# One block behind each mixer: attention of a head between the half groups of the next heads' query projection

## What is computed

```python
x = x + mix                                   # mix ends in a product with the mixer's wo
q = (rmsnorm(x, norm_xattn) @ xa_wq)          # four heads of 256
p = softmax(q @ mk.T * 256 ** -0.5)           # over 256 memory tokens, for each head
x = x + (p @ mv) @ xa_wo
h = rmsnorm(x, norm_ffn)
x = x + (silu(h @ w1) * (h @ w3)) @ w2
```

## Time and profile before

| | |
|---|---|
| median of three runs | 3963.66 us (3962.3 to 3965.55) |
| profiled execution, its time | 3961.41 us |
| its span, first to last instruction | 3959.6 us |
| mean granted clock of PE, of full speed | 0.944 |
| PE busy | 3509.9 us, 89% |
| DVE, ACT, POOL busy | 39%, 28%, 15% |

### The profile page before, as it was taken

How to read it: one execution, slowest core, us unless ns; L and a number is a source line. 1 busy time by engine, 2 the same in 40 slices (tenths; PEclk the granted TensorE clock), 3 DMA queues, 4 the chain that set the end, 5 groups by cost and what they waited for, 6 DMA issues and landing times. The chain is left out here.

```text
span 3959.6 us, 62416 instructions
## 1 busy us (share of the span) xinstructions
PE 3509.9 (89%) x26745; PEld 3302.5 (83%) x26745; DVE 1546.4 (39%) x2408; ACT 1124.8 (28%) x2089; POOL 603.4 (15%) x859
## 2 busy tenths in 40 slices
PE   9899576986999999998899884765987999999998
PEld 8888465976999999996598784664986999999997
DVE  6345433333332232235326667445324333232233
ACT  6223235212321121124535521444302321121123
POOL 2000030100210010012312357320100111010011
PEclk9999797998999999998899997897998999999999
DMA  7322101221211111113656576854121211111111
GB/s 229 86 64 65 74 17 53 65 83 55 43 49 49 43 49 48 44 44 111 211 164 209 194 187 133 214 122 108 52 94 44 59 43 49 48 44 49 44 44 64
DMA packets 479601, 340.98 MB, mean 86 GB/s; under 512 B 108142, under 2 KB 455502, under 8 KB 476078
## 3 DMA queue, kind: packets, MB, share of 16 engines
q1 hardware_dynamic: 425082, 298.49, 26.4%
q10 hardware_dynamic: 43876, 18.99, 1.9%
q0 software_dynamic: 10368, 19.51, 1.5%
HBM read 241.40 MB, written 95.61 MB: 85 GB/s over the span
## 5 line engine op out<-in xcount | busy, mean ns | idle before, releaser
L83 PE MATMUL ps<-ff_h,ff_wh 128*128 128x352 f32 x4224 | 1009.3, 322 | 0.0
L83 PEld LDWEIGHTS ps<-ff_h,ff_wh 128*128 128x128 f32 x4224 | 730.3, 188 | 1.3
L83 PE MATMUL ps<-y_parts,ff_wh 128*128 128x352 f32 x2880 | 694.7, 323 | 16.9 <-DVE ff_wl L1069 16.9
L83 PE MATMUL ps<-ff_h,ff_wl 128*128 128x352 f32 x2112 | 676.5, 320 | 0.0
L83 PEld LDWEIGHTS ps<-y_parts,ff_wh 128*128 128x128 f32 x2880 | 504.5, 189 | 17.2 <-DVE ff_wl L1069 17.2
L83 PE MATMUL ps<-y_parts,ff_wl 128*128 128x352 f32 x1440 | 466.0, 324 | 0.0
L83 PEld LDWEIGHTS ps<-ff_h,ff_wl 128*128 128x128 f32 x2112 | 396.0, 187 | 0.0
L1213 DVE TENSOR_TENSOR x<-ps,x 128x352 f32<-128x352 f32 x240 | 125.8, 524 | 483.8 <-PE ps L83 480.9
L1453 POOL TENSOR_TENSOR ff_silu<-ff_silu,rs 128x352 f32<-128x352 f32 x132 | 126.8, 962 | 1229.5 <-ACT ff_silu L1392 1229.5
L83 PE MATMUL ps<-rw_parts,rw_wh 128*128 128x352 f32 (+1 forms) x1152 | 289.6, 333 | 25.4 <-PEq L2502 13.7
L83 PEld LDWEIGHTS ps<-y_parts,ff_wl 128*128 128x128 f32 x1440 | 271.8, 189 | 0.0
(11 more groups left out here) (370 smaller groups left out, 5462.5 us busy)
## 6 DMA issues: line engine op xcount, KB each, us to landing
ff_w<-in_ffn_w SPq DMA_DIRECT2D x120, 512.0 KB, 3.8
mixed_t<-oq_st SPq DMA_DIRECT2D x48, 176.0 KB, 1.9
rw_ra_d<-tb_rk SPq DMA_DIRECT2D x8, 1056.0 KB, 8.2
rw_kbt_d<-tb_gk SPq DMA_DIRECT2D x8, 1056.0 KB, 4.0
rw_gg_d<-tb_gk SPq DMA_DIRECT2D x8, 1056.0 KB, 6.1
fr_w<-in_xa_wk SPq DMA_DIRECT2D x8, 1024.0 KB, 5.4
fr_w<-in_xa_wv SPq DMA_DIRECT2D x8, 1024.0 KB, 5.4
oq_w<-in_xa_wq SPq DMA_DIRECT2D x16, 512.0 KB, 4.1
```

The source lines that it names most:

```text
L83: mm = nc.tensor.matmul(out, l, part, start=start and n == 0, stop=stop and n == 2)
```

## The change

All blocks behind a mixer become one (`after_mixer`), with one weight stream of wo, xa_wq, xa_wo and the feed-forward. The split of y goes tile by tile at the block's start, beside the first weight loads, and the first unit of wo takes the tiles in that order (`sum_across`). q stays on chip, in the space of y, and so do the keys and values of both memories, loaded when wo is done. The attention is cut in 20 steps: a head and 256 prompt tokens (four per head), or a head and the 32 sample tokens. A slot n turns step n-2, makes the scores of step n and the values of step n-2. Slots of the first three heads stand between the half groups (12 matmuls) of the xa_wq units of later heads, at the half groups listed in `slots`; those of the last head stand behind xa_wq, with the split of the finished heads' results (`z_high`, `z_low`) and the first unit of xa_wo between them. The result banks of the weight stream are four instead of six; the other four are for the attention.

The core of the diff:

```diff
+    def sum_across(self, pe, j, rhs, ready):
+
+        w = self.weights
+        pe.wait_ge(w.lows, j + 1)
+        for b in range(BLOCKS):
+            at, before = self.place(j, b)
+            if before:
+                pe.wait_ge(self.emptied[at], before)
+        for k in range(KT):
+            pe.wait_ge(ready, k + 1)
+            for n, (weight, part) in enumerate(((w.wh, rhs[0]), (w.wh, rhs[1]), (w.wl, rhs[0]))):
+                for b in range(BLOCKS):
+                    mm = self.nc.tensor.matmul(self.bank(j, b), weight[:, j % 2, k, :], part[:, k, columns(b)],
+                                               start=k == 0 and n == 0, stop=k == KT - 1 and n == 2)
+                    if k == KT - 1 and n == 2:
+                        mm.then_inc(self.done, 1)
...
+        with nc.sbuf_tensor(f"xq{l}", [P, KT, TOK], F32, side="right") as q, \
+                nc.sbuf_tensor(f"xmem{l}", [P, 2, 2, mt * D], F32, side="right") as mem:
+            pass
+        y2 = ctx.enter_context(nc.sbuf_tensor(f"am{l}_y", [P, 2, KT, TOK], F32R, side="right"))
+        mix.close()
+        ctx.enter_context(nc.cleanup_on_exit())
...
+        units = [(lambda dst, u=u, w=w: w(u, dst), KT)
+                 for w in (wo, plain(a["xa_wq"][l]), plain(a["xa_wo"][l])) for u in range(KT)]
...
-        groups = Groups(nc, ctx, name, ps, units)
+        groups = Groups(nc, ctx, f"am{l}", ps, units, ring=4)
...
+        def step(n):
+
+            h, c = divmod(n, STEPS)
+            return (h, 0, 2, P, c * 2 * P) if c < PAIRS_ else (h, 1, 1, DEC, SEQ)
+
+
+        slots = {12 * (n // STEPS + 1) + (1, 3, 6, 8, 11)[n % STEPS]: n for n in range(LAST_HEAD)}
+        HALVES = 6 * KT
 
...
-                if j == KT:
+                if j == QU + 2:
+                    sp.wait_ge(groups.done, BLOCKS * KT)
+                    for w in range(2):
+                        for i in range(2):
+                            sp.dma_start(by_row(mem[:, w, i]),
+                                         sources[w][i][l, 0].rearrange("(t p) h d -> p t (h d)", p=P)).then_inc(mem_in, 16)
...
+            def turn_keys(w):
+                if w == 0:
+                    pe.wait_ge(mem_in, 64)
+                    pe.wait_ge(norm.logs, BLOCKS)
...
+            def scores(n):
+                h, w, chunks, tok, t0 = step(n)
+                if n == 0:
+                    pe.wait_ge(k_copied, 8)
+                groups.wait_emptied(pe, QU + 2 * h + 1, (t0 + chunks * tok - 1) // BLK)
+                if n >= 2:
+                    pe.wait_ge(exped, n - 1)
+                for c in range(chunks):
...
+            def turns(n):
+                _, _, chunks, tok, _ = step(n)
+                pe.wait_ge(probs, n + 1)
+                if n:
+                    pe.wait_ge(p_copied, n)
+                else:
+                    pe.wait_ge(k_copied, 8)
...
+            def meets(n):
+                h, w, chunks, tok, _ = step(n)
+                m = chunks * tok
+                pe.wait_ge(p_copied, n + 1)
+                if n:
+                    pe.wait_ge(o_out, n)
...
+            def slot(n):
+                if n >= 2:
+                    turns(n - 2)
+                if n < N:
+                    scores(n)
+                if n >= 2:
+                    meets(n - 2)
+
+            groups.sum_across(pe, 0, y, y_lows)
+            for j in range(1, QU):
                 for b in range(BLOCKS):
                     groups.sum(pe, j, b, y)
+            for i in range(HALVES):
+                j, b, half = QU + i // 6, i // 2 % BLOCKS, i % 2
+                if j == QU and half == 0:
+                    norm.wait_parts(pe, b)
+                groups.sum(pe, j, b, z, half * KT // 2, (half + 1) * KT // 2)
+                if j == QU and half:
+                    norm.total(pe, b, ps[:, 4 + b % 2, 0:BLK])
+                if i in (7, 9):
+                    turn_keys(i // 9)
+                if i in slots:
+                    slot(slots[i])
+            for n in range(LAST_HEAD, N + 2):
+                slot(n)
+                if LAST_HEAD + 3 <= n < LAST_HEAD + 3 + BLOCKS:
+                    if n == LAST_HEAD + 3:
+                        pe.wait_ge(z_lows, KT - 2)
+                    groups.sum(pe, XO, n - LAST_HEAD - 3, z, 0, KT - 2)
+            pe.wait_ge(o_out, N)
+            for b in range(BLOCKS):
+                groups.sum(pe, XO, b, z, KT - 2, KT)
+            for j in range(XO + 1, FF):
+                for b in range(BLOCKS):
+                    groups.sum(pe, j, b, z)
...
+            for k in range(KT):
+                nc.scalar.activation(y[0][:, k], ys[k], ACT.Copy).then_inc(y_highs, 1)
+                if k < 2:
+                    weights.high(act, k)
...
+            for i in range(HALVES):
+                if i % 6 == 0 and i:
+                    weights.high(act, QU + i // 6 + 1)
+                if i in slots:
+                    slot(slots[i])
+            for n in range(LAST_HEAD, N + 2):
+                slot(n)
+                if n < LAST_HEAD + 3:
+                    z_high(2 * (n - LAST_HEAD))
+                    z_high(2 * (n - LAST_HEAD) + 1)
+                if n == LAST_HEAD + 2:
+                    weights.high(act, XO + 1)
...
+            def leave(n):
+                h, _, chunks, tok, t0 = step(n)
+                m = chunks * tok
+                out = ps[:, 7, 0:2 * m].rearrange("p (d t) -> p d t", d=2)
+                tiles, at = slice(2 * h, 2 * h + 2), slice(t0, t0 + m)
+                dve.wait_ge(o_done, n + 1)
+                if n < LAST_HEAD:
+                    nc.vector.tensor_copy(q[:, tiles, at], out).then_inc(o_out, 1)
+                else:
+                    nc.vector.tensor_copy(z[0][:, tiles, at], out).then_inc(last_high, 1)
+                    dve.wait_ge(last_high, n - LAST_HEAD + 1)
...
+            def slot(n):
+                if 1 <= n <= N:
+                    divide(n - 1)
+                if n < N:
+                    before(n)
+                if n >= 2:
+                    leave(n - 2)
...
-                for b in range(BLOCKS):
-                    onto(x, groups, dve, j, j, b)
-                    norm.low(dve, j, b)
+                norm_tiles(norm, j, j)
+            for i in range(HALVES):
+                j, b = QU + i // 6, i // 2 % BLOCKS
+                if i % 6 == 0:
+                    weights.low(dve, j + 1)
+                if i % 2:
...
+                if n < LAST_HEAD + 3:
+                    z_low(2 * (n - LAST_HEAD))
+                    z_low(2 * (n - LAST_HEAD) + 1)
+                if n == LAST_HEAD + 2:
+                    weights.low(dve, XO + 1)
+            for j in range(XO, FF):
+                if j > XO:
```

More of the change, by code:

```diff
@@ L84, in three_passes @@
     return mm
[L87 to L99, removed]
 def plain(w, first=0):
@@ new lines, in turned, with z_high @@
+            def turned(n):
+                _, _, chunks, tok, _ = step(n)
+                act.wait_ge(p_turned, n + 1)
+                nc.scalar.activation(pt[:, 0:mt * chunks * tok], ps[:, 6, 0:mt * chunks * tok], ACT.Copy).then_inc(p_copied, 1)
+            def slot(n):
+                if n >= 2:
+                    turned(n - 2)
+                if n < N:
+                    exps(n)
+            def z_high(k):
+                act.wait_ge(o_out, STEPS * (k // 2 + 1))
+                act.wait_ge(groups.done, BLOCKS * XO)
+                nc.scalar.activation(z[0][:, k], q[:, k], ACT.Copy).then_inc(z_highs, 1)
@@ new lines, in _ @@
+            weights.high(act, QU + 1)
+            for b in range(BLOCKS):
+                norm.scale(act, b, ps[:, 4 + b % 2, 0:BLK])
+            for i in range(HALVES):
[10 more added lines that the diff above has]
+                    weights.high(act, XO + 1)
@@ new lines, in slot, with z_low, norm_tiles @@
+            def slot(n):
+                if 1 <= n <= N:
+                    divide(n - 1)
+                if n < N:
+                    before(n)
+                if n >= 2:
+                    leave(n - 2)
+            def z_low(k):
+                dve.wait_ge(z_highs, k + 1)
+                nc.vector.tensor_tensor(z[1][:, k], q[:, k], whole(z[0][:, k]), ALU.subtract).then_inc(z_lows, 1)
+            def norm_tiles(norm_, j, u):
+                for b in range(BLOCKS):
+                    onto(x, groups, dve, j, u, b)
+                    norm_.low(dve, u, b)
@@ new lines, in _ @@
+            for i in range(HALVES):
[3 more added lines that the diff above has]
+                if i % 2:
+                    groups.wait_summed(dve, j, b)
+                    norm.wait_scale(dve, b)
+                    groups.frees(nc.vector.tensor_tensor(q[:, j - QU, columns(b)], groups.bank(j, b), rs[:, columns(b)],
+                                                         ALU.mult), j, b)
+                if i in (7, 9):
+                    copy_keys(i // 9)
+                if i in slots:
+                    slot(slots[i])
@@ L1419, in _ @@
```

(9 more changed lines are left out.)

425 lines of the change are left out of this document (131 added, 294 removed).

## The result

The changed kernel takes **3830.6 us** (median of four runs, 3826.8 to 3835.6) against 3963.0 in the same comparison: a ratio of 0.9668, with a 95% interval of 0.9656 to 0.968. That is 132 us less; the forecast was 124 less, 3840 in a range of 3820 to 3885. The profiled execution took 3826.76 us with a span of 3825.0, 134.6 less than the span before.

The account below looks back on a forecast made before the run. PE bounds every projection, so only its idle and low-clock time can be won: 52.6 + 51.9 + 12.7 + 11.2 = 128.4, less 4.4 for slots, gives 124 us off the median: 3840 us, range 3820 to 3885.

Parts of the forecast that it names:

- The start: Start of the block: weight load issued beside y's split, so PE starts 12.7 us earlier in layer 0, 11.2 in layer 1.
- The attention in PE's queue: Attention of the slots up to wq's last matmul: 54.2 us of PE work, all on the path.
- the slots' waits: 44 slots of both layers: half groups between cover the softmax, 0.1 us each, 4.4 us; bounds 0 and 41.
- The chain: In a slot, scores to probabilities through DVE and ACT: 3 us in all, covered by half groups of 3.8 or 5.8.
- the lock-step rival: Slots do not overlap and PE stands 1.97 us in each, 87 us instead of 4.4: 3922 us; chance 0.11.
- The tail: Last head behind wq with xa_wo's first unit: 37.2 us PE work plus 10 standing, 47 us a layer.
- The memory: Keys and values loaded after wo: 15.8 us, wanted 17.2 us later; cost 0, bound 4.4 a layer plus 2 for restart.
- the ring: Weight stream's result banks, six to four: a bank is wanted again 11.5 us later; cost nothing, in the feed-forward too.
- The clock rival: wq's slots and tail: chopped PE work lowers the clock; at half of it 154 us, 3994 us; chance 0.05.

Follow-up runs that it names:

- old_start: Kernel after, with only the start undone: all of y is split first and the weights are loaded after that; 3854.0 us, ratio 0.9721.
- ends: behind_wq with block ends as waits: memory loaded after wq, xa_wo's weights after the attention, its first unit not between last slots; 3895.6 us, ratio 0.9832.
- behind_wq: Kernel after, with all slots moved behind wq and the lag of two steps kept; 3833.3 us, ratio 0.9672.
- scores_twice: Kernel after, with every step's scores made twice into the same bank; 3876.7 us, ratio 0.978.
- depth0: Kernel after, with scores, turning and values of the same step in one slot; 4054.9 us, ratio 1.0228.
- depth1: Kernel after, with slots still inside wq but the lag taken from two steps to one; 3895.5 us, ratio 0.9824.
- behind_depth1: Kernel after, with slots behind wq and a lag of one step; 3922.3 us, ratio 0.9894.
- behind_direct: Kernel after, with all slots but the first two behind wq and DVE splitting every result straight into xa_wo's input; 3815.5 us, ratio 0.9625.
- ring3: Kernel after, with three result banks for the weight stream instead of four; 3830.0 us, ratio 0.9675.

## Why the prediction was right, and where its reasons were not

The gain of 132 us, taken apart by runs: 21 for the start (old_start), 63 for the ends of the blocks around the attention (ends against behind_wq), 2 for the place inside wq, and 46 that is left between ends and before (67 us) less the start. These 46 would be the old rounds' own standing, the sample's round by itself and the way of q through main memory, which no run tests or separates; and the four parts are added as if they did not touch each other, which no run with two of them undone shows.

**The start: right.** Forecast 12.7 and 11.2 us; from the first issue to the first matmul it is 6.8 and 7.6 us, against 19.4 and 18.65; and with the old order alone 21 to 23 come back.

**The attention in PE's queue: right in kind, mis-sized.** It is billed one for one, as scores_twice shows. From the first matmul of wo to wq's end it is 239.5 us, 51.6 over the 187.9 of before; the forecast had 54.2 and 2.2 for the slots. This term is 4.8 us too large in layer 0 and, in the same way, 4.3 in layer 1, which is all of the 8 us by which the forecast fell short. A slot takes 3.70 us where the sum had 0.53 + 1.85 + 1.85 and 0.1. The prices came from groups of matmuls divided by their count (3.69 / 16 = 0.23), and such a group's duration holds the pipeline's end after the last one. From start to start a slot's eight scores take 766.60 − 764.87 = 1.73, 0.216 each. And the slots' waits, taken at 0.1 each, are nothing in wq.

**Why the slots do not wait: the reason was not enough.** The prediction put it to the "two or three half groups (3.8 or 5.8 us)" between slots, against a chain of 3 us from scores to probabilities. The chain was right: PE stands 2.96 us for it in depth0, where nothing covers it (the 3.7 and 3.9 us of the later expectations were too long). But depth1 has these half groups, and PE stands 1.1 to 1.4 us in ten places of wq, because the sum left out where the division stands in DVE's queue; with the division written earlier, seven of the ten go. And behind_wq has no half groups, and PE stands there once, 1.24 us, before the tail. What covers in the kernel after is the lag of two steps, which the prediction named in half a sentence ("the slot before or the one before that") without weighing it. That the slots came out without waits is luck as far as the reason goes: the one given would not have held them at a lag of one. The argument for the lock-step rival (DVE in order, a wait on a group's last matmul ahead of other work) is what bites at a lag of one, though there it is the division that is late: behind the projection's result, and in three places behind the next weight's low part. The rival's price of 1.97 us a round, 87 us in all, was far too low for the full lock step: depth0 costs 222.

**The tail: right, 47.0 and 47.1 us for 47,** with the idles on ACT's copy that it named. That it is so close is partly luck, two errors that cancel: PE's work is 40.0 with the pipeline's ends, not 37.2, and it stands 7.6, not 10.

**The memory and the ring: right.** The first of the four loads is issued at 719.37, the last at 721.41, and that one lands 11.5 us later, at 732.9; PE wants the keys at 736.28. That is 13.5 us against 16.9, 3.4 of margin, where the forecast had 15.8 against 17.2; in ends, where nothing covers it, the same load costs 12.8. Ring of four: cost 0, and of three too.

**The clock rival: right to be a rival.** The forecast held against it that idles of 1.36 and 0.31 left the clock at 0.93. For idles of that size this held: with 1.1 to 1.4 us in ten places of wq (depth1, 735 to 870 us) and with 1.29 to 2.16 in each slot (behind_depth1, 830 to 900 us) the clock is 1.00. With 2.96 and 0.69 in each slot (depth0) it is 0.81, and the time is over that of before. In the kernel after the rival did not come since there are no idles in wq; longer ones would not have been harmless.

## What to carry to other kernels

When a softmax or another chain through slower engines has to hide behind a full matrix engine, count the steps between making scores and using them; a lag of two steps hid a chain of about 3 us here wherever the work stood, and weaving it into other matmuls added 2 us, less than the noise. Ask which waits stand ahead of a short operation in its engine's queue: the same chain, unchanged in length, cost PE 1.1 to 1.4 us in ten slots a layer because its division was written behind other work. Then look at ends of blocks: loads, transposes and first weights that wait for an end were half of this gain, and a buffer that is free earlier in another order (behind_direct) was worth 17 us more.

## What the runs showed of the hardware that was not expected

Idles of about the same size had different effects on the clock. In the tail of the kernel after, PE stands 1.10, 1.90 and 2.85 us within 15 us, and the granted clock of the stretch is 1.00; ring3 has the same tail, and with 1.10, 1.91 and 1.20 its clock is 0.89 from 880 to 895 us; in behind_wq's attention, whose idles sum to 7.2 us, it is 0.97, and 0.83 from 875 to 895. In behind_depth1, 14 idles of 1.29 to 2.16 us, one a slot, leave it at 1.00; a stretch of it, and PE's waits for the division in its layer 0 (us, times, longest):

```profile
864.00:880.00 16.00, 10.97 (x57) 8.47 (x57) 5.95 (x16) 4.18 (x14) 0.00 (x0) 1.00 0.00 0
```

```profile
PE ps L1185 <- DVE xpr L1364: 41.3, 18, 5.8
```

In the tail behind them, with three idles of 4.65 to 5.78 us, it is 0.67 to 0.84, and in depth0, with 2.96 and 0.69 in every slot, it is 0.81. What decides between these cases is open. In depth0 this costs 89 us, two thirds of what the idles themselves cost.
